# The first FFN's 24 sum copies are issued by ScalarE inside mLSTM heads 1 to 3, instead of by SyncE between the weight loads

## What is computed

```python
def trunk(x, ...):
    h = concat(meta, x)
    for i in range(2):
        xn = rmsnorm(h, norm_mix[i])
        h = h + (mlstm_mixer if i == 0 else diff_attn)(xn, ...)
        xn = rmsnorm(h, norm_ffn[i])
        h = h + swiglu(xn, ffn_w_in[i], ffn_w_out[i])

def mlstm_mixer(xn, w_in, b_gate, g_head, w_out):
    proj = xn @ w_in                    # q, k, v, o and gates, 4 heads
    h = mlstm_cell(q, k, v, ig_f, lf_f) + flip(mlstm_cell(flip(q), ...))
    return (rms(h, g_head) * sigmoid(o)) @ w_out

def swiglu(xn, w_in, w_out):
    g, u = split(xn @ w_in)
    return (silu(g) * u) @ w_out
```

## Time and profile before

| | us |
|---|---|
| median of 3 executions | 1908.65 (1906.99 to 1910.79) |
| the profiled execution, own time | 1908.87 |
| its span, first to last instruction | 1907.0 |
| TensorE busy | 1880.2 (99%) |
| VectorE, ScalarE, GpSimd busy | 1241.4, 870.1, 1165.7 |
| mLSTM heads 0 to 3 with what is around them | up to about 359 |
| output projection of the mLSTM | about 359 to 440 |

### The profile page before, as it was taken

The page is one execution under the profiler, slowest core; times in us unless marked ns, Lnnn a source line. Parts: engine busy times, 40 slices in busy tenths (PEclk is TensorE's granted clock), DMA queues, the critical chain, the costliest instruction groups (busy, mean ns, idle before and its releaser), DMA issues.

```text
span 1907.0 us, 31586 instructions
## 1 busy us (share of the span) xinstructions
PE 1880.2 (99%) x10881; PEld 1750.9 (92%) x10881; DVE 1241.4 (65%) x2148; ACT 870.1 (46%) x1837; POOL 1165.7 (61%) x1537
## 2 busy tenths in 40 slices
PE   8999999999999999999999999999999999999999
PEld 7888887899999999999988888888889999999998
DVE  7756465667757565656776666666488575756673
ACT  6333333335544444445524444444465454544453
POOL 4533524376877777788853333333358787887885
PEclk9999999999999999999999999999999999999999
DMA  5559999697466978763366666656124435353534
GB/s 164 183 194 258 231 257 240 172 198 171 114 204 214 281 219 273 225 184 108 113 137 127 128 122 125 126 116 117 57 84 122 133 111 150 97 153 103 153 115 129
DMA packets 378985, 305.39 MB, mean 160 GB/s; under 512 B 14259, under 2 KB 322262, under 8 KB 378598
## 3 DMA queue, kind: packets, MB, share of 16 engines
q1 hardware_dynamic: 348304, 233.69, 40.6%
q0 software_dynamic: 28416, 69.21, 20.0%
q10 hardware_dynamic: 2134, 0.82, 0.2%
HBM read 298.88 MB, written 143.20 MB: 232 GB/s over the span
## 4 chain that ended last, share of the span: by engine, by line
PE 89%; DVE 6%; DMA 2%; ACT 1%; issue 1%; POOL 1%; ACTq 0%; DVEq 0%; SPq 0%; POOLq 0%
PE ps L922 50%; PE ps L829 24%; PE ps L1075 3%; PE ps L1236 3%; PE ps L1204 2%; DMA raw<-in_m_w_out_dram 2%; PE ps L1055 1%; PE ps L1226 1%; PE ps L1138 1%; POOL wl L726 1%; DVE rstd L1422 1%; DVE sx L1474 0%; PE ps L1168 0%; PE ps L1329 0%; PE ps L1040 0%
## 5 line engine op out<-in xcount | busy, mean ns | idle before, releaser
L922 PE MATMUL ps<-sx,wh 128*128 128x400 f32 (+1 forms) x2044 | 530.3, 340 | 0.9 <-POOL wl L756 0.5
L756 POOL TENSOR_TENSOR wl<-raw,wh 128x256 fp32r<-128x256 f32 (+1 forms) x432 | 352.5, 840 | 100.1 <-ACT wh L2141 98.7
L722 POOL CAST wh<-raw 128x256 fp32r<-128x256 f32 x252 | 105.2, 465 | 492.4 <-PE ps L829 443.8
L922 PEld LDWEIGHTS ps<-sx,wh 128*128 128x128 f32 x2044 | 373.4, 188 | 2.7 <-ACT gt_first L2156 0.9
L922 PE MATMUL ps<-sx,wl 128*128 128x400 f32 (+1 forms) x1022 | 347.6, 340 | 0.0
L756 POOL TENSOR_TENSOR wl<-raws,wh 128x256 fp32r<-128x256 f32 x328 | 285.2, 890 | 85.8 <-ACT wh L2141 84.8
L1633 DVE TENSOR_TENSOR h<-h,ps 128x400 f32<-128x400 f32 (+1 forms) x280 | 154.6, 559 | 132.5 <-PE ps L922 132.4
L922 PE MATMUL ps<-fx,wh 128*128 128x400 f32 (+1 forms) x904 | 235.3, 341 | 0.1
L829 PE MATMUL ps<-xh,wh 128*128 128x512 f32 (+1 forms) x752 | 215.9, 363 | 0.0
L829 PE MATMUL ps<-xl,wh 128*128 128x512 f32 (+1 forms) x752 | 207.4, 349 | 0.0
L726 POOL TENSOR_TENSOR wl<-raw,wh 128x256 fp32r<-128x256 f32 x252 | 198.9, 817 | 5.2
(11 more groups left out here) (309 smaller groups left out, 3588.4 us busy)
## 6 DMA issues: line engine op xcount, KB each, us to landing
in_sums<-in_ffn_w_in_dram SPq DMA_DIRECT2D x16, 1536.0 KB, 9.2
raw<-in_sums SPq DMA_DIRECT2D x96, 256.0 KB, 3.0
in_sums<-in_ffn_w_in_dram SPq DMA_DIRECT2D x16, 1280.0 KB, 8.2
raw<-in_ffn_w_in_dram SPq DMA_DIRECT2D x80, 256.0 KB, 3.0
raws<-in_sums SPq DMA_DIRECT2D x80, 256.0 KB, 3.0
raw<-out_sums SPq DMA_DIRECT2D x120, 128.0 KB, 2.4
raws<-in_ffn_w_in_dram SPq DMA_DIRECT2D x52, 256.0 KB, 3.1
raw<-in_m_w_in_dram SPq DMA_DIRECT2D x24, 512.0 KB, 4.6
```

The source lines that it names most:

```text
L722: ins = pool.tensor_copy(wh[:, slot, c], raw[:, slot, c])
L756: ins = pool.tensor_tensor(slot_of(n, 1)[:, c], raw_of(n)[:, c], slot_of(n, 0)[:, c].bitcast(F32), ALU.subtract)
L922: mm = pe.matmul(product_bank(layer, s, j), slot_of(n, low_w)[:, k * P:(k + 1) * P], x, start=(j in OPENS and k + q == 0), stop=(k == tile ...
```

## The change

`copy_for_sum` moves out of SyncE's program and takes the queue that issues it. SyncE keeps only the weight loads in this stage (the second FFN's copies stay on SyncE, inside the first FFN). ScalarE's program gets five places in a head where it issues copies: behind the copies out of PSUM, behind `values`, behind the state weights of the longer sequence, behind its squares, and behind the state weights of the shorter one. The loop over heads 1 to 3 is written out.

```diff
+        def copy_for_sum(queue, layer, i):
+
+            part, which = divmod(i, 4)
+            unit = N_PART * layer + part
+            if which == 0 and unit > 1:
+                queue.wait_ge(sums_copied[unit % 2], 64 * (unit // 2))
+            row, col = ((1, 0), (0, 0), (0, 0), (0, 1))[which]
+            queue.dma_start(sum_columns(layer, (0, 2, 1, 3)[which], part),
+                            weight_columns(layer, row, col, part)).then_inc(sums_copied[unit % 2], 16)
...
                 for j in range(6):
                     n = MIX0 + hd * 6 + j
                     weights(n, j % 2, mlstm_cols(hd, j))
-                    if hd == 1 and j < 4:
-                        copy_for_sum(0, 2 * j)
-                        copy_for_sum(0, 2 * j + 1)
-                    else:
-                        copy_for_sum(0, n - 2)
             for j in range(2):
                 weights(OUT0 + j, j, cols(m_w_out[0], j * P))
-                copy_for_sum(0, OUT0 + j - 2)
...
-            def mlstm_head(hd, n, first=False):
+            def mlstm_head(hd, n, first=False, copies=((),) * 5):
...
+                for c in copies[0]:
+                    copy_for_sum(sc, 0, c)
...
                 for j in OF_SEQ[0]:
                     if j == (1 if first else 4):
                         values()
+                        for c in copies[1]:
+                            copy_for_sum(sc, 0, c)
                     decays(j)
...
                 for j in OF_SEQ[0]:
                     state_weights_high(j)
+                for c in copies[2]:
+                    copy_for_sum(sc, 0, c)
                 for i in OF_SEQ[0]:
                     squares(i)
+                for c in copies[3]:
+                    copy_for_sum(sc, 0, c)
                 for j in OF_SEQ[1]:
                     decays(j)
                 for j in OF_SEQ[1]:
                     state_weights_high(j)
+                for c in copies[4]:
+                    copy_for_sum(sc, 0, c)
...
-            with sc.Fori(0, M_HEADS - 1) as i:
-                mlstm_head(i + 1, i * 6 + (MIX0 + 6))
+            copies = {1: ((0, 1, 2, 3), (4, 5), (6, 7), (8,), (9,)), 2: ((10,), (11,), (12,), (13, 14), (15,)),
+                      3: ((16,), (17, 18), (19, 20), (21, 22), (23,))}
+            for hd in range(1, M_HEADS):
+                mlstm_head(hd, MIX0 + 6 * hd, copies=copies[hd])
```

More of the change, by code:

```diff
@@ L592, in attn_cols @@
                 return cols(d_w_in[0][:, of * D:(of + 1) * D], c)
[L594 to L602, removed]
             def factor(layer, n):
@@ L631, in ffn_factors @@
                     if layer == 0 and j == 0 and 10 <= s < 34:
-                        copy_for_sum(1, s - 10)
+                        copy_for_sum(sp, 1, s - 10)
             def first_weights(j):
```

## The result

The change makes the kernel slower. Median of four executions 1929.13 us (1926.95 to 1932.12), against 1909.72 us (1906.99 to 1911.49) for four of the kernel before on the same chip: ratio 1.0102 [1.009, 1.0114]. The prediction was 1922 with a range of 1912 to 1936, and 0.91 for slower. The medians stand 19.4 us apart.

What follows compares the result with a forecast made beforehand. TensorE was taken as the bound, busy 1880 of 1907 us, so transfers matter only through its waits. Terms 5.9 + 0 + 1.4 + 6 = 13.3 us on 1908.9 gave 1922 us, range 1912 to 1936.

Steps and rivals of the forecast that it cites:

- What the change removes: SyncE's 24 copy issues, in heads and output projection: claimed to cost nothing, so gain 0, at most the two waits.
- the rival at 1902: Output projection: its two loads are slow because of SyncE's earlier queue, so both waits and clock losses go; chance 0.04.
- A: Head 1: add 0 waits for copies 0 to 3, delaying block 10; 4.4 us wait plus 1.5 clock, 5.9 us.
- B: Head 1: add 2 waits for copies 4 to 7, with block 12's split behind it; 0 us, other bound 3.2.
- The later parts have room: After add 2: later copies come ahead of need, copy 11 by 6 us, copies 12 to 15 by some 20 us.
- C: Heads 2 and 3: copy issues on ScalarE delay the shorter sequence's exponentials; 0.7 us each, 1.4 us, bounds 0 and 12.5 more.
- D: Output projection: leftover copies 19 to 23 and add 15 collide with the reload of `h` and load 26; 6 us, bounds 0 and 9.
- the pile-up of delays: Rival: A 10, B 3.2, C 1.4 + 6, D 9, giving 1939 us, values around 1930 included; chance 0.22.
- Only head 1 pays: Rival: A and C cost time, D is hidden because loads may be served ahead of the leftover; 1916 us, chance 0.28.

## Why the prediction was right, and where its sizes were off

**What the change removes: 0, right.** The early copies on ScalarE and the written-out loop both measure as no change, so neither SyncE's issues nor the loop had anything to give. That the two old waits stem from SyncE's copies (the rival at 1902) falls with the first of these: it takes all copies off SyncE, and the two waits stay, at 3.6 us.

**A, 5.9 us: right in mechanism, 1 us short.** Add 0 stood at 149.4 by the working and at 150.1 on the chip; TensorE waited 4.7 us for 4.4. The clock cost 2.5 us for 1.5, since TensorE worked 5.6 us at the lower level, not 3.4. Head 2 starts 7.0 us late, up to 8.4 in other profiles of the same stretch.

**B, 0: right for block 12, wrong for the sentence behind it, "The later parts have room".** Block 12 was ready at 194.1 and needed at 195.3. The working gave the block's own due time and stopped there (add 2 went out at 187.9, between its 183 and 190). It left out that the load of block n + 2 waits for split n: with split 12 22 us late, the load of block 14 lost 22 us of lead and then took 26.7 us beside copies 8 and 9 and the adds. This cost 3.5 us of waiting and 1.5 of clock, of the 6.0 us that head 2's stage grew. The run with copies 8 and 9 later shows the second half (18.2 us, no wait), the run with late adds the first. It is the largest term that the sum lacked. For the later adds alone there was room, as foreseen: GpSimd stood 9.4 us at add 8 and 8.9 at add 10, and TensorE waited for neither.

**C, 1.4 us: mechanism named, size wrong.** "With ScalarE's queue holding only copies I expect little of that" was the failing step. The queue did hold ScalarE, 3.3 us at copy 22, and head 3 lost 3.9 us where 0.7 were foreseen; in head 2, 0.4. The 3.9 us is shown by the kernel in which 21 and 22 stand behind the exponentials. The bound of 12.5 us had covered it.

**D, 6 us: the wait was seen, but its net is not above what executions differ by (1.1 us).** The 14 us of moving that the working multiplies stand in no row (it had 16.5 us itself, which would have given +8); the +6 from the leftover does not need them, but rests on 253 GB/s, and the stretch from 306 to 376 then moved 277. The load of block 26 took 20.5 us for 22 foreseen and 16.1 before, the wait before block 26 grew by 4.1, not 6, and its clock cost by 0.6 (4.7 us at the lower level for 3.4). What the sum did not count is that the wait at block 29 and its clock, 3.7 us, went; why is open. That the loads catch up while TensorE waits does not fit two of the runs, where block 26 waited 10.0 and 10.7 and block 29 still 3.4 and 1.8. Net 1.1 us. The size is no constant: 9 to 11 us of waiting in front of block 26 in five of the experiments, 5.5 in a sixth, 0.2 with the loads ahead. What sets it within this spread was not isolated; adds or copies pushed to a later time went with the larger values in four of the five.

**The sum.** 13.3 foreseen; 7.0 + 6.0 + 3.9 + 1.1 = 18.0 of 18.1 measured. A sum 5 us short: the heads were 9.6 us too small, and that D was 4.9 too large took half of this back. This was luck, not working. The median of 1929 is "around 1930", which the prediction had given to the pile-up of delays. Of its conditions one came true, the queue that holds ScalarE in head 3; the others (block 12 late, A of 10 us) did not. So the time lies between the forecast and that rival in cause as well as in number. "Only head 1 pays" (1916) falls with head 2's 6.0 us.

**Why the lateness costs at all.** Before, copies filled a stretch that had room; now they do not. Windows of after, 60 to 125 and 306 to 376, the last figures being clock, DMA share and GB/s:

```profile
60.00:125.00 65.00, 63.49 (x387) 51.91 (x386) 46.09 (x128) 29.21 (x66) 23.59 (x36) 1.00 0.12 33
306.00:376.00 70.00, 66.57 (x395) 54.68 (x394) 37.56 (x108) 21.81 (x54) 27.73 (x45) 0.98 1.07 277
```

The first of these windows had a share of 0.61 at 211 GB/s before. The second had 0.91 at 213 GB/s, and head 2 had 1.00 at 253. The work has left the first and has gone into stretches where the DMA engines were busy nearly all the time already.

## What to carry to other kernels

Moving an issue to another engine's queue at the same time was free here; moving it later was not, so ask for the due time of each transfer, and also for what stands behind the engine that waits for it: its next job, and the load that this job sets free. An issue cost its engine little here while few copies were outstanding, and 3 to 10 us when it was held; put it where the engine would idle anyway. A stretch with idle DMA engines ahead of a saturated one is worth something: here, work taken out of it came back as waits in and behind the saturated one.

## What the runs showed of the hardware

- An issue on ScalarE's queue was held although nothing but copies was in that queue: copy 22 in head 3 for 3.3 to 4.8 us in five kernels, with three copies of 1.3 or 1.5 MB outstanding, copies 4 and 5 in head 0 for 5.3 us behind four, and copy 10 in head 2 for 10.15 us behind two. ScalarE does nothing meanwhile ("3.46 <-issue").
- A 512 KB load, from block 11's on, took 3.7 to 19.7 us before and 7.0 to 29.1 with the change; the longest are those of blocks 14 and 15, 26.7 and 29.1. With part 5 on SyncE a load took 44.4 us and a 1280 KB copy 42.7, the time at the hand-over (4.8 and 17.0) within. In a quieter stretch of before, a copy took 11.8.
- Behind some waits of TensorE the clock fell to 1.2 GHz. At waits of 1.7 to 3.9 us it was low for 3.4 or 6.8 us or not at all, at those of 4.2 to 6.4 us for 6.8, at those of 9.1 to 11.5 for 10.2 or 13.7. The longer stretches begin within the wait, so that TensorE worked at the lower level for about 3 to 6 us; at 45% this is 1.4 to 2.8 us on top of the wait.
- At short waits the fall is no certainty. In the kernel with early copies on ScalarE the clock stayed up behind waits of 1.9, 1.7 and 2.9 us, and with the adds later behind one of 3.1. The third wait of the early copies, and the time behind it:

```profile
440.65:443.57 2.92, 0.00 (x1) 0.00 (x1) 2.05 (x3) 2.34 (x5) 2.86 (x4) 1.00 1.03 269
443.57:447.00 3.43, 3.43 (x19) 3.43 (x20) 3.43 (x6) 3.08 (x8) 2.23 (x3) 1.00 0.55 153
```

So a term for the clock behind a short wait has to carry 0 as a bound; that bound the prediction had.
